# A hybrid decoder trunk: output gates computed as feature tiles between the attention's chunks, and the scores' levels summed to one

## The reference

```python
h = rmsnorm(x, n1);  z = h @ w_in                      # z = [u | q | f | i | gate], each 512 wide
y_pool = pool_mix(z[..., :512], ...)                   # running means over windows 2, 4, 8, 16, then w_pool
q = silu(q) * 128 ** -0.5                              # hgrn2_mix, 4 heads of 128
k = (1 - lb) * sigmoid(-f);  v = i;  log_f = ...
A = einsum('nhtd,nhsd,nhtsd->nhts', q, k, exp(G[t] - G[s]))     # causal; G = cumsum(log_f)
o = A @ v + (q * exp(G)) @ S
S = exp(G_last) * S + (k * exp(G_last - G)).T @ v
o = o * rsqrt(mean(o * o) + EPS) * g_norm              # per head
y_rec = o * silu(gate)
x = x + concat(y_pool, y_rec) @ w_out
x = x + (gelu(conv(h2 @ w_a)) * (h2 @ w_b)) @ w_down    # h2 = rmsnorm(x, n2)
y = rmsnorm(x, final_g)
```

## Time and profile before

| what | value |
|---|---|
| median of three runs | 2874.8 us |
| profiled execution | 2871.09 us |
| its span | 2869.2 us |
| TensorE busy | 2614.6 us, 91% |
| VectorE busy | 1202.9 us, 42% |
| ScalarE busy | 697.0 us, 24% |
| GpSimd busy | 440.4 us, 15% |
| mean granted TensorE clock | 0.955 of full speed |

### The profile page before, as it was taken

How to read it: one execution, slowest core, us unless ns; L and a number is a source line. 1 busy time by engine, 2 the same in 40 slices (tenths; PEclk the granted TensorE clock), 3 DMA queues, 4 the chain that set the end, 5 groups by cost and what they waited for, 6 DMA issues and landing times.

```text
span 2869.2 us, 34984 instructions
## 1 busy us (share of the span) xinstructions
PE 2614.6 (91%) x12479; PEld 2132.6 (74%) x12479; DVE 1202.9 (42%) x2344; ACT 697.0 (24%) x1389; POOL 440.4 (15%) x316
## 2 busy tenths in 40 slices
PE   5977786999889998899999998899999998899997
PEld 4865665888767787688877787688877787688776
DVE  5624844444524548422224548321224746322224
ACT  2211302222222333211122323211122422211123
POOL 3420332455545102000000002000000011000000
PEclk8986898999989999999999999899999999999999
DMA  4542023666666651355564641355555631355553
GB/s 146 192 160 88 8 97 113 225 237 220 237 224 230 254 209 45 118 185 188 188 217 181 238 173 44 121 189 190 189 221 193 246 125 60 147 190 190 209 194 137
DMA packets 142288, 489.07 MB, mean 170 GB/s; under 512 B 8897, under 2 KB 75697, under 8 KB 92840
## 3 DMA queue, kind: packets, MB, share of 16 engines
q1 hardware_dynamic: 133689, 482.67, 47.1%
q10 hardware_dynamic: 8472, 4.75, 0.6%
HBM read 375.54 MB, written 112.02 MB: 170 GB/s over the span
## 4 chain that ended last, share of the span: by engine, by line
PE 64%; DMA 8%; DVE 6%; issue 4%; ACT 2%; SPq 1%; DVEq 0%; POOL 0%; ACTq 0%
PE ps L493 20%; PE ps L495 20%; PE ps L494 20%; DMA w_split<-w_both 8%; PE ps L621 1%; DVE arena L1647 1%; PE ps L647 1%; ACT arena L972 1%; SPq L370 1%; DVE arena L1615 1%; PE ps L525 0%; DVE x_tok L1709 0%; DVE arena L1614 0%; DVE h_lo L1367 0%; DVE arena L1359 0%
## 5 line engine op out<-in xcount | busy, mean ns | idle before, releaser
L493 PE MATMUL ps<-h_hi,w_both 128*128 128x512 f32 (+1 forms) x1888 | 746.9, 396 | 19.2 <-DVE x_tok L1709 8.9
L495 PE MATMUL ps<-h_lo,w_both 128*128 128x512 f32 (+1 forms) x1888 | 739.2, 392 | 0.0
L494 PE MATMUL ps<-h_hi,w_both 128*128 128x512 f32 (+1 forms) x1888 | 736.0, 390 | 0.0
L493 PEld LDWEIGHTS ps<-h_hi,w_both 128*128 128x128 f32 x1888 | 360.7, 191 | 97.6 <-issue 21.8
L495 PEld LDWEIGHTS ps<-h_lo,w_both 128*128 128x128 f32 x1888 | 360.4, 191 | 81.5
L494 PEld LDWEIGHTS ps<-h_hi,w_both 128*128 128x128 f32 x1888 | 361.1, 191 | 78.8
L493 PE MATMUL ps<-w_both,act_hi 128*128 128x512 f32 (+1 forms) x748 | 301.2, 403 | 27.2 <-DVE act_lo L1782 27.2
L495 PE MATMUL ps<-w_both,act_hi 128*128 128x512 f32 (+1 forms) x748 | 299.2, 400 | 0.0
L494 PE MATMUL ps<-w_both,act_lo 128*128 128x512 f32 (+1 forms) x748 | 298.3, 399 | 0.0
L1782 DVE TENSOR_TENSOR act_lo<-arena,act_hi 128x512 fp32r<-128x512 f32 (+1 forms) x176 | 133.5, 762 | 342.9 <-ACT act_hi L1255 342.9
L328 POOL TENSOR_TENSOR arena<-arena 128x256 f32<-128x256 f32 x56 | 40.5, 723 | 1511.8 <-DVE arena L1615 1511.8
(11 more groups left out here) (238 smaller groups left out, 2924.0 us busy)
## 6 DMA issues: line engine op xcount, KB each, us to landing
w_both<-w_split SPq DMA_DIRECT2D x288, 1024.0 KB, 4.8
w_split<-w_both SPq DMA_DIRECT2D x96, 1024.0 KB, 6.2
w_raw<-in_w_down SPq DMA_DIRECT2D x24, 512.0 KB, 4.2
w_raw<-in_w_a SPq DMA_DIRECT2D x22, 512.0 KB, 4.3
w_raw<-in_w_b SPq DMA_DIRECT2D x22, 512.0 KB, 4.3
w_raw<-in_w_in SPq DMA_DIRECT2D x20, 512.0 KB, 4.3
x_tok<-in_x_prompt SPq DMA_DIRECT2D x16, 512.0 KB, 6.7
arena<-in_x_prompt SPq DMA_DIRECT2D x16, 512.0 KB, 5.6
```

The lines of the kernel that those rows point to most:

```text
L493: nc.tensor.matmul(out, lhs[0], rhs[0], start=first, stop=False)
L494: nc.tensor.matmul(out, lhs[1], rhs[0], start=False, stop=False)
L495: return nc.tensor.matmul(out, lhs[0], rhs[1], start=False, stop=last)
```

## The change

The gates become feature tiles, like u. Their four units move behind those of u in the order of units; each tile is put behind a chunk of the attention (in block 0 the first one stands just before the attention). ScalarE copies them out of PSUM into the space of `g_t`, head by head as that is no longer needed, and takes the silu of all four behind chunks 10 to 13, with one table load before and one after. The values V stand directly behind Q. A chunk's output is now copied to SBUF by ScalarE (`o_tok`), squared from there, and no longer multiplied by VectorE; the copy alone frees the PSUM tile. After the attention the outputs are scaled by the root alone, transposed, and one VectorE instruction per tile multiplies the transposed tile in PSUM by the gain (now a column) and the gate (`gated`); ScalarE and VectorE then split the result as before, from SBUF. VectorE sums all eight masked score matrices in one reduction, and one matmul with the values is left. The pooling products move to chunks 12 to 15, in block 0 as well. `gn` is no longer loaded by itself; its gain comes with the `vectors`.

```diff
-U_F, U_Q, U_GATE, U_V, U_U, U_OUT, U_UP, U_DOWN = 0, 4, 8, 12, 16, 20, 28, 72
+U_F, U_Q, U_V, U_U, U_GATE, U_OUT, U_UP, U_DOWN = 0, 4, 8, 12, 16, 20, 28, 72
...
-U_BEHIND = {g: g + 1 for g in range(HEADS - 1)}
-POOLED_BEHIND = {0: 0, 1: 1, 2: 2, 11: 3}
-PRODUCT_BEHIND = {10 + g: g for g in range(HEADS)}
-LOW_BEHIND = {11 + g: g for g in range(HEADS)}
+U_BEHIND = {0: 1, 2: 2, 4: 3}
+POOLED_BEHIND = {0: 0, 1: 1, 3: 2, 10: 3}
+GATE_BEHIND = ({5: 0, 7: 1, 8: 2, 10: 3}, {2: 1, 6: 2, 10: 3})
+SILU_BEHIND = {10: 0, 11: 1, 12: 2, 13: 3}
+PRODUCT_BEHIND = {12 + g: g for g in range(HEADS)}
+LOW_BEHIND = ({13: (0,), 14: (1,), 15: (2, 3)}, {12 + g: (g,) for g in range(HEADS)})
...
-        gate = part(6720, TILES + 1, 512)
+        o_tok = part(6720, TILES + 1, 512)
+        gate_t = g_t
+        yg = part(11840, TILES, 512)
...
-        a_sum = part(21086, 4 * P)
+        a_sum = part(21086, P)
...
# TensorE, a chunk's outputs
-                        pe.wait_ge(o_squared, n)
-                        pe.wait_ge(o_gated, n)
-                    for l in range((1 + LEVELS) // 2):
-                        nc.tensor.matmul(o, a_sum[:, win(l)], v_tok[:, w, hc], start=l == 0, stop=False)
+                        pe.wait_ge(o_taken, n)
+                    nc.tensor.matmul(o, a_sum, v_tok[:, w, hc], start=True, stop=False)
...
-                    if not hd and i in PRODUCT_BEHIND:
-                        pool_product(b, PRODUCT_BEHIND[i])
+                    if i in GATE_BEHIND[hd]:
+                        gate_tile(b, hd, GATE_BEHIND[hd][i], i + 1)
+                    if i in PRODUCT_BEHIND:
+                        pool_product(b, hd, PRODUCT_BEHIND[i], i + 1)
...
             def u_tile(b, g):
                 if g >= 2:
                     pe.wait_ge(u_taken, 4 * b + g - 1)
+                else:
+                    pe.wait_ge(v_taken, 4 * b + 3 + g)
                 feature_tile(b, U_U + g, g, 6 + g % 2, None, 0)
...
+            def gate_tile(b, hd, g, chunks):
+                if g < 2:
+                    pe.wait_ge(u_taken, 4 * b + (4 if hd else 3 + g))
+                else:
+                    pe.wait_ge(gate_taken, 4 * b + g - 1)
+                feature_tile(b, U_GATE + g, g, 6 + g % 2, 4, hd, win(2 + g % 2).start, chunks)
...
-                token_tiles(b, U_GATE, (4, 5, 6, 7), 2, hd)
+                token_tiles(b, U_V, (4, 5, 6, 7), 2, hd)
                 pe.wait_ge(q_taken, 4 * b + 4)
-                token_tiles(b, U_V, (0, 1, 2, 3), 4, hd)
-                pe.wait_ge(gate_taken, 4 * b + 4)
...
# TensorE in block 0, behind head_attention
-                    for g in range(HEADS):
-                        pe.wait_ge(pooled_ready, g + 1)
-                        if g >= 1:
-                            pe.wait_ge(pool_taken, g)
-                        nc.tensor.matmul(ps[:, g % 2, :], wp[:, g, :], pooled[:, g, HEAD:WIDE], start=True, stop=True)
-                        nc.tensor.matmul(ps[:, 2, 0:HEAD], wp[:, g, :], pooled[:, g, 0:HEAD], start=True,
-                                         stop=True).then_inc(pool_done, 1)
-                    pe.wait_ge(pool_taken, 4)
...
+                    gate_tile(0, 1, 0, 0)
                 attention(b, hd)
...
# ScalarE: values taken without a table load, gate and silu as functions
-                nc.scalar.preload_act_table(ACT.Silu)
-                act.wait_ge(unit_done, UNITS * b + U_GATE + 4)
-                for t in range(TILES):
-                    nc.scalar.activation(gate[:, t, :], ps[:, 4 + t, :], ACT.Silu).then_inc(gate_taken, 1)
-                nc.scalar.preload_act_table_set("natural_log_exp_and_others")
                 act.wait_ge(unit_done, UNITS * b + U_V + 4)
                 for t in range(TILES):
-                    nc.scalar.copy(v_tok[:, t, :], ps[:, t, :]).then_inc(v_taken, 1)
+                    nc.scalar.copy(v_tok[:, t, :], ps[:, 4 + t, :]).then_inc(v_taken, 1)
+                def take_gate(g):
+                    act.wait_ge(unit_done, UNITS * b + U_GATE + g + 1)
+                    act.wait_ge(eg_ready, 4 * b + g + 1)
+                    nc.scalar.copy(gate_t[:, g, HEAD:WIDE], ps[:, 6 + g % 2, :]).then_inc(gate_taken, 1)
+                def silu(g):
+                    act.wait_ge(gate_taken, 4 * b + g + 1)
+                    nc.scalar.activation(gate_t[:, g, lo:WIDE], gate_t[:, g, lo:WIDE], ACT.Silu).then_inc(gate_ready, 1)
...
                 if hd:
+                    take_gate(0)
                     decays(b, 1, range(1 + LEVELS))
...
                     act.wait_ge(o_done, n + 1)
-                    nc.scalar.activation(o_junk[:, :], ps[:, 4, 0:P], ACT.Square,
+                    nc.scalar.copy(o_tok[:, w, win(h)], ps[:, 4, 0:P]).then_inc(o_taken, 1)
+                    act.wait_ge(o_taken, n + 1)
+                    nc.scalar.activation(o_junk[:, :], o_tok[:, w, win(h)], ACT.Square,
                                          accum_out=osumsq[:, w, h:h + 1]).then_inc(o_squared, 1)
                     if not hd and i in U_BEHIND:
                         take_u(U_BEHIND[i])
                     if i in AHEAD:
                         decays(b, *AHEAD[i])
+                    if i in GATE_BEHIND[hd]:
+                        take_gate(GATE_BEHIND[hd][i])
+                    if i == min(SILU_BEHIND) - 1:
+                        nc.scalar.preload_act_table(ACT.Silu)
+                    if i in SILU_BEHIND:
+                        silu(SILU_BEHIND[i])
+                    if i == max(SILU_BEHIND):
+                        nc.scalar.preload_act_table_set("natural_log_exp_and_others")
...
# VectorE, a chunk
-                    v.tensor_tensor(a_sum, a_all[:, 0:4 * P], a_all[:, 4 * P:8 * P], ALU.add).then_inc(at_ready, 1)
+                    v.tensor_reduce(a_sum, a_all.rearrange("p (l t) -> p t l", t=P), mybir.AxisListType.X,
+                                    ALU.add).then_inc(at_ready, 1)
...
-                    dve.wait_ge(o_squared, n + 1)
-                    v.tensor_tensor(gt, gt, ps[:, 4, 0:P], ALU.mult).then_inc(o_gated, 1)
...
# VectorE, mixer_output
-                        last = v.scalar_tensor_tensor(out=gt, in0=gt, scalar=orstd[rows, 4 * t + h:4 * t + h + 1],
-                                                      in1=gn[rows, :], op0=ALU.mult, op1=ALU.mult)
+                        last = v.tensor_scalar(ot, ot, orstd[rows, 4 * t + h:4 * t + h + 1], None, ALU.mult)
...
+                def gated(t):
+                    dve.wait_ge(yt_done, 4 * b + t + 1)
+                    v.scalar_tensor_tensor(out=yg[:, t, :]..., in0=ps[:, 6 + t % 2, :]..., scalar=gcol,
+                                           in1=gate_t[:, :, main(t)], op0=ALU.mult, op1=ALU.mult).then_inc(yg_ready, 1)
+                gated(0)
                 for t in range(TILES):
+                    if t + 1 < TILES:
+                        gated(t + 1)
                     dve.wait_ge(y_hi, 4 * b + t + 1)
-                    v.tensor_tensor(h_lo[:, 4:8, main(t)], ps[:, 6 + t % 2, :]..., h_hi..., ALU.subtract)
+                    v.tensor_tensor(h_lo[:, 4:8, main(t)], yg[:, t, :]..., h_hi..., ALU.subtract)
```

137 lines of the change are left out of this document (75 added, 62 removed).

## The result

The changed kernel takes 2888.5 us (median of 5 runs, 2888.43 to 2895.28) against 2874.9 of the kernel before: ratio 1.0046, 95% interval 1.0033 to 1.0059. It is 13.7 us slower. The forecast was 2845, from 2818 to 2868, with 0.11 for slower. The execution that was profiled took 2895.3 us (span 2893.5), 6.8 above the median; a second one (experiment e1) had a span of 2889.1. What both traces show is told as the kernel's; where they differ, both numbers are given.

What follows compares the result with a forecast made beforehand. TensorE, busy 91%, was taken as the main bound, with waits on VectorE and ScalarE in the attention. Blocks 1 to 3 (-11) and block 0 (-18.5) gave -29.5 on 2871.1, 2841.6; the median's 3.7 made 2845 us, range 2818 to 2868.

Steps and rivals of the forecast that it cites:

- the first stage: Blocks 1 to 3 before the attention: four gate units leave, less a wait for V's copies and clock loss; -16.2 us each.
- I take 1.64: Length of VectorE's new reduction per chunk: 1.64 us, a cost per output, between ends of 1.21 and 1.90.
- rival 2: The reduction is slow because its inputs lie 512 B apart: 2.3 us each, kernel at 2864 us; chance 0.13.
- The stretch by GpSimd: Reduction beside GpSimd's exponents: taken as not lengthened; if lengthened like the add, about 5 us in all.
- The chunk table: Attention of blocks 1 to 3, TensorE time chunk by chunk: sum 96.7 us against 85.56, 11 us lost.
- (a): Block 0 ahead of V: the gate's four units leave, so everything behind starts 28 us earlier.
- (b): Block 0's head attention: VectorE no longer waits for the squares to gate; -2 us net of GpSimd's splitting.
- (c): Block 0's start behind the head attention: pooling products go, gate tile and decays stand in line, 27 us for 35.5; -8.5.
- (d): Block 0's chunks: gate tiles, late products and reduction add, hidden stalls and spared value products give back; about 91 us, +18.5.
- (e): Block 0 after the attention: output stage grows by 1.5 us.
- number 3: Block 0 keeps less: lined-up waits and splitting eat 10.5 us, chunks 8 more; 2863 us, chance 0.1.
- number 4: Slower: the reduction makes VectorE bound every chunk, deciding from about 2.8 us each; 2903 us at 3.5, chance 0.1.

Runs made afterwards that it cites:

- e1: The changed kernel run once more with nothing edited: 2887.6 us.
- b2: The changed kernel with 18 extra unread matmuls filling TensorE's wait for V's copies in blocks 1 to 3: 2879.3 us.
- a3: The changed kernel with the reduction reading its eight inputs side by side, not 512 B apart (outputs wrong, timing only): 2870.0 us.
- b4: The kernel of b3 with the masking writing its matrices interleaved, so the reduction reads side by side: 2852.5 us.
- a1: The changed kernel with the old sum, one add and four value products, instead of the reduction and one product: 2886.2 us.
- b3: The changed kernel with the first u tile in bank 3, pooling products one chunk earlier, and blocks 1 to 3's output transposes between the output units: 2855.6 us.
- d4: The changed kernel with extra unread matmuls filling the waits in block 0's head attention: 2881.9 us.
- c2: The kernel of b3 with block 0's pooling products back behind chunks 12 to 15 and head 1's decays before the first gate tile's copy: 2843.3 us.
- d1: The kernel of c2 with three adds for the reduction and block 0's output transposes before its second output unit: 2830.4 us.

## Why the prediction was wrong, step by step

The sum was -29.5 us on the profiled execution; the two profiled executions differ by +24.3 (19.9 with e1's), the medians by +13.7. The stages below are those of the profiled pair and account for its 53.8 us; 10.5 of these are no error of the sum, since the one execution lay 3.7 us below its median and the other 6.8 above. The steps that failed are the length of the reduction, the clock behind the waits, and in block 0 the head attention and the credit for the spared value products. Two of the prediction's own signs of being wrong came: the reduction over 1.9 us and the attention over 101.

**Stage by stage in blocks 1 to 3.** The gate's units left as forecast (13 units of 5.56), and the wait for V's copies was 4.35 us where 4.5 were forecast. Mis-sized is the clock behind it: 1.5 charged, 3 measured (b2: 5.7 us at half clock, 2.85). In the first trace block 2 has 3.4 us at half clock at its start as well, which neither the kernel before nor e1 has there: another 1.3. That is the step "the first stage": -16.2 forecast, -13.5 to -14.9 measured.

**The reduction.** The step "I take 1.64" failed: 1.95, outside both ends (1.21 and 1.90), because the stride costs, as rival 2 said; a3 shows it, 1.22 without, and 18.5 us less for the kernel (rival 2 had put the stride at 19). From the head rows' reduction of five inputs per output, 192 B apart, three readings were made, and the one by inputs (0.67 ns each) was the nearest. The Trainium skill (SBUF — State Buffer, Door 1: The DMA port swizzle, box on cachelines) has each step to a new line of 16 B pay a penalty; a3 and b4 agree, where 512 B and 32 B apart cost 0.73 and 0.84 us on 1024 elements. For the forecast, the 0.31 us over 1.64 are worth some 8 us of the kernel (an estimate: 0.31 of a3's 0.73, of its 18.5 us), by proportion 1.7 in each later block. Against the old sum the reduction is no loss to speak of (2 us, a1), since it spares TensorE three of four value products in each chunk, and tiles cover part of it. The stretch by GpSimd did not come: 1879 to 2027 ns over all 64, where the add went to 2703. That part held.

**The attention of blocks 1 to 3.** The chunk table was right within 0.3 us in most of its lines: chunks 3, 5, 6 and 10 were given 6.4, 9.8, 3.0 and 9.1 us and took 6.66, 9.70, 3.18 and 9.34 in the trace. Two failed. Chunk 4 was given 8.1 and took 9.83, of which 1.5 is half clock behind the wait of 2.34 us: in a3, where this wait is 1.67 us, there is no dip, and the chunk takes 8.32; so it does in block 1 of e1, behind the same 2.34 us. And the chunks 14 and 15 with the wait for the last `pool_low` were given 5.5 and took 6.95 (5.91 in a3, so that 1 us of it is the reduction's). The sum was 96.7 against 101.9.

**After the attention.** +1.5 forecast, +1.4 measured in block 2 up to the second output half. The chain of eight VectorE instructions was rightly seen; b3 shows that it can be covered whole, with the half clock behind it: 14 us in three blocks.

Blocks 1 to 3 come to +5.0, +4.8 and +3.1 where -3.7 was forecast for each. The 8.5 us between forecast and block 2 are the half clock behind V's copies and at the block's start (2.7 net, the wait being 0.15 shorter than charged), chunk 4 (1.7), the tail (1.45), the other chunks together (2.2) and the rest of the block (0.5): no large error, but all of one sign, in a sum whose gain was 3.7. A gain of that size, left over from 22 taken out and 16 put back, should have had a range of both signs.

**Block 0** was -18.5 and is +7.9; the letters are those of the prediction.

(a) the gate's units ahead of V, -28 forecast, -27.3 measured.

(b) the head attention, -2 forecast, +6.2 measured (100.96 to 107.18 us with the wait ahead of it; 106.7 in e1): the step "VectorE no longer waits" is true of two heads (4.78 us of idle instead of 5.70; 6.16 in the last), but the mean clock of the stage is 0.64 against 0.69, some seven tenths of its time at half clock, and the first and the last head, which had 0.73 and 0.75, no longer do better than the others. The forecast never read the clock of this stage, though the trace had it. With the waits filled (d4) the stage is 8.8 us shorter.

(c) the start behind it, -8.5 forecast, -8.2 measured, by the very line that was forecast (27.24 us for 27; 28.7 in e1). c2 shows that this line needn't be.

(d) the chunks, +18.5 forecast, +27.0 measured (29.3 in e1), although a tile takes 8.4 us at full clock (d4) and not the 9.2 charged. The sum set 3 us for the reduction against some 8 that the spared value products were to give (72.3 + 27.6 + 8 + 3 - 12 is 98.9, and it said 91): 5 to the good. But a1, which takes both back, has these chunks 1.8 us shorter (97.5), 4.2 against e1's: together they cost. That is about 7 of the 8.5 us. The reduction's part was too small: shortening it by 0.73 us took 5.6 us out of these chunks (a3), so that its 1.25 us over the old sum are worth some 10 (an estimate by proportion).

(e) after the attention, +1.5 forecast, +6.5 measured: the transposed chain waits 6.7 us in block 0; d1 takes 8 us off. The rest of block 0 was to be unchanged and grew by 3.7 (1.6 in e1, so part of it is scatter).

**Costed at nothing: the gain's row in `vectors`.** The first product of block 0 starts 3.5 us later (3.7 in e1). 2.4 to 2.6 of this stand at the first matmul, which waits for that load; where the other 1.1 come from isn't known. The Trainium skill (DMA: Bandwidth & Descriptors, Why a DMA increments its semaphore by 16 and not by 1) says that a DMA is spread over the largest number of engines up to 16 that divides its outer dimension: 16 for 112 rows, one for 113, a prime. The traces agree: the 112 transfers of 512 B lie within 0.58 us (4.98 to 5.56), up to 14 of them under way at once, the 113 follow one another, about 0.024 us apart, over 2.82 us (5.12 to 7.94; 5.28 to 7.97 in e1). The 2.2 us between the two lengths are nearly the whole of the later start. A load of 113 rows cut in two was not tried.

Of the rivals, number 2 was right in its mechanism, number 3 in its place (block 0 keeps less), and number 4, the one that forecast slower, was right in its sign and wrong in its mechanism: it was to decide from 2.8 us a reduction. What made the kernel slower was in no rival as a whole: the stride's price on top of many waits, each somewhat longer than charged, and the clock behind them.

## A version that beats both

d3 takes 2824.9 us, 49 less than the kernel before and 64 less than the changed one: the changed kernel with the first u tile in its own bank, the outputs' transposes under an output unit, the pooling products of blocks 1 to 3 one chunk earlier, decays ahead of the first gate tile in block 0, three adds for the reduction, and filled waits in the head attention. Without the fill (d1) it is 2830.4.
